# Two value units as seven block products in place of eight, their weight sums on VectorE, and modulation sums one place later

## The reference

```python
for l in range(2):
    h = x @ w_in[l]
    (hg_q, hg_f, hg_i, hg_gate, mla_cq, mla_ckv, mla_kr, mla_gate,
     mem_q, mem_gate) = jnp.split(h, IN_OFFSETS, axis=-1)
    y_hg = _hgrn2_group(hg_q, hg_f, hg_i, lower_bounds[l], hgrn_out_norm[l])   # hg_i: 1024 columns, the values
    y_mla = _mla_group(...)           # causal latent attention, 8 heads
    y_mem = _memory_group(mem_q, mem, w_mem_k[l], w_mem_v[l])
    y = jnp.concatenate([y_hg * silu(hg_gate), y_mla * silu(mla_gate), y_mem * silu(mem_gate)], axis=-1) @ w_out[l]
    x = _layernorm(ALPHA * x + y, ln_g[l], ln_b[l])
```

## Time and profile before

| | us |
|---|---|
| median of 3 runs | 1395.18 (1393.79 to 1396.9) |
| the profiled execution, whole | 1393.01 |
| its span, first to last instruction | 1391.2 |
| PE busy in the span | 1270.6 (91%) |
| DVE busy | 812.6 (58%) |
| POOL busy | 652.6 (47%) |
| ACT busy | 436.0 (31%) |

### The profile page before, as it was taken

The page is one execution under the profiler, slowest core; times in us unless marked ns, Lnnn a source line. Parts: engine busy times, 40 slices in busy tenths (PEclk is TensorE's granted clock), DMA queues, the critical chain, the costliest instruction groups (busy, mean ns, idle before and its releaser), DMA issues.

```text
span 1391.2 us, 17185 instructions
## 1 busy us (share of the span) xinstructions
PE 1270.6 (91%) x6328; PEld 784.6 (56%) x6328; DVE 812.6 (58%) x1694; ACT 436.0 (31%) x1065; POOL 652.6 (47%) x647
## 2 busy tenths in 40 slices
PE   9999999999999999999999999988787877887786
PEld 8887686648887686549655565633333333333232
DVE  0776377441566287352357774869988654444445
ACT  1533344111334334222234443333323232222223
POOL 0556667431646667432204455445444545445550
PEclk9999999999999999999999999999998989999999
DMA  9544335546444344647449999999999999999995
GB/s 373 214 167 167 136 119 216 203 160 222 157 167 183 122 160 175 247 147 269 164 174 415 421 372 421 410 422 421 421 420 422 420 422 420 421 421 421 421 420 244
DMA packets 54061, 406.77 MB, mean 292 GB/s; under 512 B 6213, under 2 KB 8666, under 8 KB 11610
## 3 DMA queue, kind: packets, MB, share of 16 engines
q0 software_dynamic: 37184, 268.45, 46.6%
q1 hardware_dynamic: 15706, 136.18, 25.5%
q10 hardware_dynamic: 1088, 1.05, 0.4%
HBM read 403.53 MB, written 1.07 MB: 291 GB/s over the span
## 4 chain that ended last, share of the span: by engine, by line
PE 35%; DMA 20%; DVE 8%; ACT 2%; issue 1%; POOL 0%; DVEq 0%; ACTq 0%; POOLq 0%
PE bank L1181 13%; DMA kM<-in_peer_uv,vM 8%; PE pj L746 7%; PE pj L782 5%; PE pj L1044 4%; PE pj L761 3%; DMA qM<-in_peer_uv,vM 3%; DMA b<-in_peer_uv,vM 2%; DMA yT<-in_peer_uv,vM 2%; DMA more_rows<-in_peer_uv,vM 2%; DMA ring<-in_peer_uv,vM 2%; DVE ring L2001 1%; DVE kM L2001 1%; ACT rope L1417 1%; PE bank L706 0%
## 5 line engine op out<-in xcount | busy, mean ns | idle before, releaser
L746 PE MATMUL pj<-xT,ring 128*128 128x256 f32 (+1 forms) x1568 | 318.4, 363 | 0.9 <-ACT hv L1351 0.4
L746 PEld LDWEIGHTS pj<-xT,ring 128*128 128x128 f32 x1568 | 276.6, 190 | 36.5 <-issue 2.6
L642 POOL TENSOR_SCALAR more_rows<-more_rows,lbt 128x256 f32<-128x256 f32 x168 | 175.7, 1046 | 16.4
L681 POOL DMA_INDIRECT ring<-in_peer_uv,vM x100 | 114.1, 1141 | 123.8 <-PE bank L1181 110.3
L2001 DVE SCALAR_TENSOR_TENSOR ring<-ring,memT 128x1024 f32<-128x1024 f32 x101 | 122.2, 1225 | 76.8 <-DMA ring<-in_peer_uv,vM 72.6
L1415 ACT ACTIVATE rope<-vM 128x1 f32<-128x1 f32 (+2 forms) x112 | 22.6, 202 | 382.0 <-DVE ring L2001 146.8
L782 PE MATMUL pj<-ring,yT 128*128 128x512 f32 x320 | 140.8, 594 | 0.0
L640 POOL TENSOR_SCALAR mod_part<-more_rows,lbt 128x256 f32<-128x256 f32 x24 | 23.8, 991 | 246.0 <-issue 121.0
L643 POOL TENSOR_TENSOR mod_part<-mod_part,more_rows 128x256 f32<-128x256 f32 x168 | 127.1, 756 | 14.0
L1181 PE MATMUL bank<-ring,tri 128*128 128x512 f32 x212 | 103.1, 631 | 24.0 <-ACT tri L1423 20.2
L1181 PE MATMUL bank<-ring,causal 128*128 128x512 f32 x188 | 90.3, 625 | 11.0 <-ACT causal L1423 11.0
(11 more groups left out here) (399 smaller groups left out, 2093.0 us busy)
## 6 DMA issues: line engine op xcount, KB each, us to landing
ring<-in_units SPq DMA_DIRECT2D x42, 2048.0 KB, 9.5
more_rows<-in_w_ada SPq DMA_DIRECT2D x24, 1024.0 KB, 4.9
ring<-in_units SPq DMA_DIRECT2D x2, 1536.0 KB, 7.7
home<-in_units SPq DMA_DIRECT2D x1, 2048.0 KB, 14.3
ring<-in_peer_uv,vM POOLq DMA_INDIRECT x100, 26.7
memT<-in_mem SPq DMA_DIRECT2D x2, 512.0 KB, 5.4
ring<-in_units SPq DMA_DIRECT2D x1, 1024.0 KB, 9.2
xT<-in_x_turned SPq DMA_DIRECT2D x1, 1024.0 KB, 11.1
```

What stands on the lines that cost most here:

```text
L642: do(g.tensor_scalar(mod_w[:, c, :], mod_w[:, c, :], silu_c[:, c:c + 1], None, ALU.mult))
L681: pool.indirect_dma_start(row_slot[k], None, d["peer_uv_2"], bass.IndirectOffsetOnAxis(ap=expert[:, t, j:j + 1], axis=0))\
L746: ins = nc.tensor.matmul(pj[s][0:n, 2 * m + first:2 * m + stop], ring[:, slot, at:at + n], act[:, c, first:stop], start=(c == 0), stop=(c ...
```

## The change

The value product of 256 x 1024 by 1024 x 1024 is cut in two along tokens (t), input channels (k) and columns (n). With x11, x12 the first 128 tokens and their two channel halves, x21, x22 the second 128 tokens, w11, w21 the two channel halves of I0 and w12, w22 those of I1, the four blocks of the result are built from seven block products in place of eight:

- sums of x, four adds on POOL before piece 2 of a layer: s1 = x21 + x22, s2 = s1 - x11, s3 = x11 - x21, s4 = x12 - s2. They lie in `home`, where the level masks move up.
- sums of weights, four adds on DVE of 128 x 2048, in place in the ring (tasks JT1 to JT4).
- products on PE, four matmuls each: J3 = s4 w22, J1 = x11 w11, J5 = s1 t1, J2 = x12 w21, J6 = s2 t2, J7 = s3 t3, J4 = x22 t4.
- combinations: one copy on ACT (JA), seven adds from PSUM on DVE (JC, JU, JV, JW).

Both units are needed from J3 and J1 on, so the units' order is now MK, C, F0, Q0, UP, F1, GM, Q1, I1, I0, G0, MQ, GE, MV, G1, O0, O2, O3, O1: MV takes the place that I1 had. I1 is counted as used up at the start of J4, I0 at its end. Four `AD` tasks in the middle of each layer stand one place later (AD4 after Y5 where it stood after Y3, AD5 after MQ, AD6 after GEa, AD7 after MV), and `LD` tasks move with the places around them. Cut to its core:

```diff
 PE_ORDER = [...
-            P1 L05 Y1 LD AD I0a P2 LD L06 LD S4 S5 P3 I0b Y2 AD Y3 AD P4 MV Y4 L07 P5 G0a L08 LD Y5 LD AD G0b MQ LD
-            AD HO0 S6 HO1 HN0 L11 GEa AD P6 S7 GEb S8 HN1 L12 LD I1 Y6 L13 P7 P8 S9 L14 Y7 G1a G1b P9 Y8 AD L15 LD L16
+            P1 L05 Y1 LD AD J3 J1 P2 LD L06 LD S4 S5 P3 J5 J2 Y2 AD Y3 P4 J6 J7 Y4 L07 P5 J4 G0a L08 Y5 AD G0b MQ LD LD AD HO0 S6 HO1 HN0 L11 GEa LD AD P6 S7 GEb S8 HN1 L12 MV LD AD Y6 L13 P7 P8 S9 L14 Y7 G1a G1b P9 Y8 AD L15 LD L16
...
-    Db04 Y0 L04 P1 Db05 Da07 S3 Db06 Y1 AD L05 P2 P3 L06 S4 P4 S5 Y2 AD P5 Db07 Y3 Da08 AD Y4 Db08 L07 Y5 L08
+    Db04 Y0 L04 P1 Db05 Da07 S3 Db06 JT1 Y1 AD L05 P2 P3 L06 S4 P4 S5 JT2 JC Y2 AD P5 JT3 Db07 Y3 JT4 Da08 JU JV Y4 Db08 L07 JW Y5 L08
...
+            def sums_of_blocks(l):
...
+                do(g.tensor_tensor(s1, x21, x22, ALU.add))
+                do(g.tensor_tensor(s2, s1, x11, ALU.subtract))
+                do(g.tensor_tensor(s3, x11, x21, ALU.subtract))
+                do(g.tensor_tensor(s4, x12, s2, ALU.subtract), "x_sums")
...
+                if piece == 2:
+                    sums_of_blocks(l)
...
+            def values_product(l, task):
...
+                elif k == 4:
+                    pe.wait_ge(sem("j_weights4"), l + 1)
+                    pe.wait_ge(sem("j_seen6"), l + 1)
+                    pe.sem_inc(sem("unit_done"), 1)
+                rows, w, dst = {3: (s4, w22, a1), 1: (x11, w11, a0), 5: (s1, w12, b0), 2: (x12, w21, b1),
+                                6: (s2, w22, a0), 7: (s3, w11, b1), 4: (x22, w21, a0)}[k]
+                for c in range(DC // 2):
+                    ins = nc.tensor.matmul(dst, rows[:, c, :], w[:, c, :], start=(c == 0), stop=(c == DC // 2 - 1))
+                if k == 4:
+                    last(ins, "unit_done")
...
-                    elif task in ("I0", "I1"):
...
-                        do(a.copy(hv[:, :, q * COLS:(q + 1) * COLS], pj[s][:, :].rearrange("p (a n) -> p a n", a=TT)),
...
+                    elif task == "JA":
+                        act.wait_ge(sem("j_product1"), l + 1)
+                        do(a.copy(hv[:, 1, COLS:], pj[1][:, 0:COLS]), "j_copied1")
...
+                            dst, first, second = ((w12, w12, w11), (w22, w22, w12), (w11, w22, w11), (w21, w21, w22))[k - 1]
+                            do(v.tensor_tensor(dst, first, second, ALU.subtract), f"j_weights{k}")
+                        elif task == "JC":
...
+                            do(v.tensor_tensor(c11, c22, pj[0][:, COLS:], ALU.add), "j_seen2")
+                        elif task == "JU":
...
+                            do(v.tensor_tensor(c21, c22, pj[1][:, 0:COLS], ALU.add), "j_seen6")
```

More of the change, by code:

```diff
@@ L116, in unit_of @@
 def unit_of(task):
+    if task in ("J3", "J1"):
+        return {"J3": "I1", "J1": "I0"}[task]
     known = task[:2] in ONE_SLOT or output_unit(task[:2])
@@ L167, in big_uses @@
             turn = 0
+        elif name == "I1":
+            out[l, "J"] = tuple(uses)
+            uses = [uses[0] + 1, uses[1] + 1]
+            turn = 0
+        elif name == "I0":
+            pass
         elif name in ONE_SLOT or name == "C":
@@ L338, in build @@
         home = sb("home", [P, DC * COLS])
[L339 removed]
+        sums_of_x = home[:, 0:16 * P].rearrange("p (k c t) -> p k c t", k=4, c=4)
+        level_mask = home[:, 16 * P:16 * P + 7 * P // 4].bitcast(u8).rearrange("p (m t) -> p m t", m=7)
         causal = sb("causal", [P, TT, T])
@@ L491, in up_weights, with value_blocks, x_blocks @@
                     w[:, UQ_W + 512:UQ_W + 1024])
+        def value_blocks(l):
+            return [ring[:, UNIT[l, name] % RING, :].rearrange("p (c n) -> p c n", c=DC)[:, half:half + DC // 2, :]
+                    for half in (0, DC // 2) for name in ("I0", "I1")]
+        def x_blocks():
+            return [xT[:, half:half + DC // 2, t * P:(t + 1) * P] for t in range(TT) for half in (0, DC // 2)]
         def ring_loads(n):
@@ L632, in _ @@
             do = steps(pool, "pool_step")
+            def sums_of_blocks(l):
+                x11, x12, x21, x22 = x_blocks()
+                s1, s2, s3, s4 = [sums_of_x[:, k, :, :] for k in range(4)]
+                if l:
+                    after(pool, "xT_ready", l - 1, 3)
+                    unit_done(pool, l - 1, "I0")
+                else:
+                    pool.wait_ge(sem("xT_load"), 16)
+                do(g.tensor_tensor(s1, x21, x22, ALU.add))
+                do(g.tensor_tensor(s2, s1, x11, ALU.subtract))
+                do(g.tensor_tensor(s3, x11, x21, ALU.subtract))
+                do(g.tensor_tensor(s4, x12, s2, ALU.subtract), "x_sums")
             pool.wait_ge(sem("silu_c"), 1)
             for j in range(N_MOD_PIECES):
+                l, piece = j // (N_MOD_PIECES // DEPTH), j % (N_MOD_PIECES // DEPTH)
+                if piece == 2:
+                    sums_of_blocks(l)
                 pool.wait_ge(sem("mod_load"), 16 * (j + 1))
@@ L869, in attention_values @@
                 last(ins)
+            def values_product(l, task):
+                x11, x12, x21, x22 = x_blocks()
+                w11, w12, w21, w22 = value_blocks(l)
+                s1, s2, s3, s4 = [sums_of_x[:, k, :, :] for k in range(4)]
+                a0, a1, b0, b1 = [pj[s][:, half * COLS:(half + 1) * COLS] for s in (1, 0) for half in range(2)]
+                k = int(task[1])
+                if k == 3:
+                    loaded(l, "I1")
+                    pe.wait_ge(sem("pj_free1"), BIG[l, "J"][1])
+                    pe.wait_ge(sem("x_sums"), l + 1)
+                elif k == 1:
+                    loaded(l, "I0")
+                elif k == 5:
+                    pe.wait_ge(sem("pj_free0"), BIG[l, "J"][0])
+                    pe.wait_ge(sem("j_weights1"), l + 1)
+                elif k == 6:
+                    pe.wait_ge(sem("j_weights2"), l + 1)
+                    pe.wait_ge(sem("j_copied1"), l + 1)
+                elif k == 7:
+                    pe.wait_ge(sem("j_weights3"), l + 1)
+                    pe.wait_ge(sem("j_seen2"), l + 1)
+                elif k == 4:
[8 more added lines that the diff above has]
+                    last(ins, "unit_done")
+                elif k != 5:
+                    last(ins, f"j_product{k}")
             def level(l, g, m):
@@ L940, in _ @@
                         channel_major(l, name, xT, COLS, part)
-                    elif name in ("I0", "I1"):
-                        token_major(l, name, xT, part)
+                    elif task[0] == "J":
+                        values_product(l, task)
                     elif name == "MK":
@@ L1707, in _ @@
                             do(v.tensor_tensor_scan(sums[:, n * P:(n + 1) * P], seg, seg, 0.0, ALU.add, ALU.bypass))
+                    elif task[0] == "J":
+                        c11, c12, c21, c22 = [hv[:, t, half * COLS:(half + 1) * COLS] for t in range(TT) for half in range(2)]
+                        w11, w12, w21, w22 = value_blocks(l)
+                        if task[:2] == "JT":
+                            k = int(task[2])
+                            if k == 1:
+                                for name in ("I1", "I0"):
+                                    dve.wait_ge(sem(f"ring_load{UNIT[l, name] % RING}"), ring_loads(UNIT[l, name]))
+                            else:
+                                dve.wait_ge(sem(("j_product3", "j_product1", "j_product2")[k - 2]), l + 1)
+                            dst, first, second = ((w12, w12, w11), (w22, w22, w12), (w11, w22, w11), (w21, w21, w22))[k - 1]
+                            do(v.tensor_tensor(dst, first, second, ALU.subtract), f"j_weights{k}")
+                        elif task == "JC":
+                            dve.wait_ge(sem("j_copied1"), l + 1)
+                            dve.wait_ge(sem("j_product2"), l + 1)
+                            do(v.tensor_tensor(c11, c22, pj[0][:, COLS:], ALU.add), "j_seen2")
+                        elif task == "JU":
+                            dve.wait_ge(sem("j_product6"), l + 1)
+                            do(v.tensor_tensor(c21, c22, pj[1][:, 0:COLS], ALU.add), "j_seen6")
+                            do(v.tensor_tensor(c12, c21, pj[0][:, 0:COLS], ALU.add))
+                        elif task == "JV":
+                            dve.wait_ge(sem("j_product7"), l + 1)
+                            do(v.tensor_tensor(c22, c12, pj[0][:, COLS:], ALU.add))
+                            do(v.tensor_tensor(c21, c21, pj[0][:, COLS:], ALU.add), "pj_free0", BIG[l, "J"][0] + 1)
+                            do(v.tensor_tensor(c12, c12, pj[1][:, COLS:], ALU.add))
+                        else:
+                            unit_done(dve, l, "I0")
+                            do(v.tensor_tensor(c21, c21, pj[1][:, 0:COLS], ALU.add), "pj_free1", BIG[l, "J"][1] + 1)
+                            dve.sem_inc(sem("hv_ready"), 2)
                     elif task[:2] == "Da":
```

10 lines of the change are left out of this document (3 added, 7 removed).

## The result

The changed kernel takes 1415.9 us (median of 4 runs, 1415.0 to 1418.3) where the kernel before took 1395.6 beside it: 1.0149 times as long, 95% interval 1.0131 to 1.0167, so 20.3 us are lost. The profiled execution has a span of 1413.0 us, 21.8 more than before; the first layer's last modulation sum (AD11) comes 10.8 us later than before and the second layer's 21.6 us (626.54 against 604.94), so the loss is made in the two layers, half in each.

A forecast was written before the change was run, and what follows sets the result against it. PE, busy in every microsecond, was taken to bound the layers, with 8.8 us of slack in POOL's circle. Each layer ends 9.7 us later, saved matmuls included; twice that, 19.4, on 1395.2 gives 1414.6 us, range 1401 to 1425.

The forecast's parts named there:

- LD5 behind MQ, MQ behind J4, landing late, POOL's circle without room: SP's queue: LD5 issued at 159.4, landing 10.0 later, piece 5 18.5 us late against 8.8 slack; layer ends 9.7 us later.
- T, the start of J4: Last value product on PE starts at 159 (bounds 155.9 to 161.5), after PE waits about 2.8 us at P2.
- A layer would gain 0.4 us: PE without the load path: reaches G0a at 162.5 against 162.96, the 3.5 us saved nearly all eaten.
- O0 waits for its load: Output products: PE waits for ring loads at O0, O2 or O3 and for POOL at AD11, some 9 us per layer.
- Weight sums at 2.8 us: Four DVE adds of 2048 elements: 2.28 us each alone, 2.8 taken beside POOL, bounds 2.28 and 4.1.
- Piece 4 ends at 152.4 and nobody waits for it: POOL's modulation pieces 3 and 4 come 6.5 us late behind I0's load; no wait yet, their PE sums being one place later.
- DVE beside POOL, "by part of an instruction": Shared port: a DVE add takes at most 0.54 us more beside POOL; the skill's whole-instruction rule would give 1417.8 us.
- Two bounds were mis-added: Six POOL pieces each 0.8 longer: +5.6 us per layer; J4's start if no sum delays PE: 155.9.
- Sums of x on POOL: Four adds ahead of piece 2, at most 5.8 us, covered by 13.05 us of POOL idling: cost nothing.
- A: Rival: piece 5 starts by 159.8, so PE's own work decides; 1388.2 us, or up to 1394; chance 0.10.
- B: Rival: sums eat the gain and POOL catches up, delays under 9 us; 1395 us, within 0.2%; chance 0.08.
- D: Rival: DVE adds of 2048 take 4.1 us, T becomes 164, 5 us more per layer; 1425 us; chance 0.02.

The follow-up runs named there:

- Experiment 10: Changed kernel with PE's new waits taken away and LD3 ahead of I0, LD5 left behind MQ: 1405.1 us, ratio 1.0066 to the kernel before.
- experiment 7: Changed kernel with only the loads moved, LD3 ahead of I0 and LD5 ahead of MQ: 1402.3 us, ratio 1.0058 to the kernel before.
- experiments 6: Changed kernel with PE's new waits taken away (first weight sum early, G1 in tile 1, two reorderings), loads left: 1408.4 us, ratio 1.0094.
- experiment 8: Changed kernel with PE's new waits taken away, LD3 ahead of I0 and LD5 ahead of MQ: 1386.8 us, ratio 0.9943 to the kernel before.
- experiment 5: Changed kernel with gate G1 in the other PSUM tile, so O0t no longer waits for ACT: 1414.6 us, ratio 1.0144.
- experiment 9: Changed kernel with LD3 alone moved ahead of I0, LD5 staying behind MQ: 1412.0 us, ratio 1.0115 to the kernel before.
- experiment 4: Changed kernel with LD5 alone issued ahead of MQ in each layer: 1410.5 us, ratio 1.0113 to the kernel before.

## Why the prediction was right, and where only its sum was

**The forecast, 1414.6 us and slower, held** (1415.9). Experiment 10 shows its mechanism by itself, in a kernel without PE's new waits and with LD3 early. In the changed kernel MQ's hold was one cause of two, and that the sum came so close is partly luck: a late piece 4 and a late PE, neither foreseen, were almost wholly hidden behind the path that was. Of its steps:

- *LD5 behind MQ, MQ behind J4, landing late, POOL's circle without room.* All there in the trace: LD5 at 162.09 with J4 at 161.74, piece 5 9.9 us after the issue (10.0 taken), AD11 behind piece 11's end at 305.32 (304.4). Two errors nearly cancel: piece 5 came 2.5 us later than forecast (171.98 for 169.5), and pieces 5 to 10, up to the start of piece 11, took 118.8 us where the forecast had 120.7.
- *T, the start of J4: 159 forecast, 161.74 measured*, outside its upper bound of 161.5. P2's wait was right to the tenth (2.82) by luck: the sum took 2.45 us of it, and the step ahead of it, 1.10 us in place of 0.69, the other 0.4. Two terms were missing: the 1.25 us by which the scores behind that wait ran slower (3.24 against 1.99 us in experiment 7), and 1.73 us in which PE waited at J4 for DVE's combination, which I had put within 0.4 us of PE's arrival.
- *"A layer would gain 0.4 us" without the load path.* **This step failed.** PE was 2.3 us late at G0a where the forecast has it 0.4 early, and 6.7 us late at O0t. Beside T, I had not seen two waits that come from places exchanged: G1 in the PSUM tile that O0t needs (2.0 us), and Y6 right behind MV, waiting for ACT's copy of it (1.0 us). POOL's path ended later still and covered all of it, which was luck; experiment 7 uncovers it.
- *O0 waits for its load.* Wrong cause: O0t waited for ACT to read G1 out of the PSUM tile. O2t and AD11 waited as forecast.
- *Weight sums at 2.8 us.* Alone they take 2.29. In the first layer they took 2.29 to 2.45, in the second one of four took 2.83. DVE's timeline after, with the step ahead of the first sum and the division ahead of the third:

```profile
129.77 1.10 DVE L1828 TENSOR_TENSOR big<-big,qT 128x512 f32<-128x512 f32 x1
130.91 2.45 DVE L1784 TENSOR_TENSOR ring<-ring 128x2048 f32<-128x2048 f32 x1
...
146.42 2.29 DVE L1784 TENSOR_TENSOR ring<-ring 128x2048 f32<-128x2048 f32 x1
...
150.52 1.16 DVE L1741 TENSOR_TENSOR sm<-sm,stat 128x512 f32<-128x512 f32 x1
151.71 2.45 DVE L1784 TENSOR_TENSOR ring<-ring 128x2048 f32<-128x2048 f32 x1
...
156.64 2.40 DVE L1784 TENSOR_TENSOR ring<-ring 128x2048 f32<-128x2048 f32 x1
```

- *Piece 4 ends at 152.4 and nobody waits for it.* **This step failed too**: it ended at 160.63, and LD5, which needs the one buffer, waits for it. I had priced what POOL does to DVE and not what DVE does to POOL. POOL's add at 146.63 began 0.2 us into a sum and took 2.67 us where it takes 0.72: it ended 0.6 us behind the sum's end (148.71). The steps at 152.55 and 156.99 show the same.
- *DVE beside POOL, "by part of an instruction".* DVE loses as well, by what POOL's step has left. Three POOL steps of after:

```profile
129.40 0.92 POOL L676 TENSOR_TENSOR mod_part<-mod_part,more_rows 128x256 f32<-128x256 f32 x1
...
150.41 0.72 POOL L676 TENSOR_TENSOR mod_part<-mod_part,more_rows 128x256 f32<-128x256 f32 x1
151.23 1.24 POOL L675 TENSOR_SCALAR more_rows<-more_rows,lbt 128x256 f32<-128x256 f32 x1
```

DVE's step at 129.77 began when POOL's add had 0.55 us left, and lost 0.41; the division at 150.52 met one with 0.61 left, and lost 0.47; the sum of 2.83 us one with 0.69 left, and lost 0.54. So beside an add DVE waited for all but the last 0.14 us. The 0.54 us that I took from the earlier trace rows for a part of an instruction is the same wait. Beside POOL's multiply it loses less: the sum at 151.71 began with 0.76 us of one left, and lost 0.16. The Trainium skill ("SBUF — State Buffer", section "SBUF: two separate sides") says that a DVE operation with two SBUF inputs and a GpSimd operation that reads SBUF lock each other out for a whole instruction. On POOL's side, and on DVE's beside adds, this trace agrees to within 0.14 us; on DVE's side beside multiplies it does not.
- So of the 21.0 us by which piece 5 is late, 14.8 were there already at the end of piece 4 (LD3 behind I0 and the stretched pieces), MQ's hold added 1.4, the landing behind a unit 4.8. The forecast gave all to MQ's hold and the landing. Either cause alone is nearly enough (experiments 6 and 10), which is why LD3 or LD5 moved alone brings 3.9 or 5.4 us and both bring 13.6.
- Two bounds were mis-added, without weight in the forecast: six pieces of 0.8 us more make 4.8 us, not 5.6, and T without any sum is 156.05, not 155.9.
- *Sums of x on POOL* cost nothing, as said: four adds of about 1.3 us before piece 2, which still waited 7.03 us for PE.

**The rivals.** A (faster, PE alone) needs more than piece 5 in time: experiment 7 grants that and is still slower than before; only experiment 8 gives A's time (1386.8 for 1388.2). B and D did not occur.

## What to carry to other kernels

When work is moved on a full engine, follow two things for every step: what is queued behind a waiting load on the same DMA-issuing engine, and which buffer each later step now falls into. A path that ends last hides the others: price each path by itself, and expect a repair of one to give only the distance to the next. A long two-input DVE instruction beside a chain of short GpSimd steps delayed that chain by 1.5 to 2.0 us each time here, for 2.3 to 2.5 us of its own, so put such sums where GpSimd idles.

## What the runs showed of the hardware that I had not expected

The clock after a wait. A single execution of each kernel is profiled. In the changed kernel the granted clock behind P2's wait of 2.82 us was 0.50, that is 1.2 of 2.4 GHz, in the next 2 us; in experiment 5, behind a wait of 2.81 us at the same place, it stayed at 1.00. The rows of the stretch, after and then experiment 5 (columns as in the earlier trace rows):

```profile
138.00:140.00 2.00, 2.00 (x18) 1.67 (x15) 1.46 (x2) 1.09 (x2) 0.00 (x0) 0.50 1.12 471
```

```profile
138.00:140.00 2.00, 2.00 (x13) 1.77 (x12) 1.73 (x3) 0.88 (x1) 0.00 (x0) 1.00 1.06 451
```

Likewise the scores behind 2.24 us at P2 took 1.99 us in experiment 7, and behind 2.25 us 3.67 in experiment 9; J4 behind 1.73 us of waiting took 3.67 us after the change and 5.37 in experiment 4 (granted clock 0.56 from 163 to 165 us); and O0t behind 1.99 us took 7.10 us after the change, behind 2.02 us 8.80 in experiment 4 (0.56 from 262 to 264 us). So a wait of 1.7 to 2.8 us on PE cost its length, or 1.2 to 1.7 us on top of it, and its length alone does not tell which.
